# Moving part of a small projection from one norm's wait to another's, and widening a layer norm's statistic

## The reference

```python
for i in range(2):
    h += 0.5 * post1(swiglu_1(pre1(h)))           # 1024 -> 2816 -> 1024
    h += post2(mixer(pre_m(h)) @ w_o)             # three branches, one with a layer norm
    h += 0.5 * post3(swiglu_2(pre2(h)))
    gate = sigmoid(pre3(h) @ w_ple_gate)          # 1024 x 1024
    h += post4((p[i] @ w_ple_proj) * gate)        # p: the embedding, 320 x 256
y = final(h)
# the mixer's third branch: silu(layernorm(dwconv31(glu))) @ w_cf_out
```

## Time and profile before

| | |
|---|---|
| three runs, median | 1551.94 us |
| the profiled execution | 1550.16 us, its span 1548.2 us |
| TensorE matmuls | 1531.0 us busy, 99% |
| VectorE, ScalarE, GpSimd busy | 67%, 46%, 42% |
| TensorE's granted clock, mean | 0.997 |
| moved by DMA | 229.31 MB, 148 GB/s |

### The profile page before, as it was taken

One profiled execution on the slowest core, in us unless ns is written; L12 is line 12 of the kernel. 1 busy time (PEld: TensorE's weight loads), 2 busy tenths in 40 slices (PEclk: granted clock), 3 DMA queues, 4 the chain that ended last, 5 costly groups with the idle time before them and its releaser, 6 DMA issues.

```text
span 1548.2 us, 28024 instructions
## 1 busy us (share of the span) xinstructions
PE 1531.0 (99%) x10408; PEld 1521.9 (98%) x10408; DVE 1034.7 (67%) x1588; ACT 713.4 (46%) x1057; POOL 643.5 (42%) x680
## 2 busy tenths in 40 slices
PE   9999999999999999999999999999999999999997
PEld 9999999999999999999999999999999999999997
DVE  7655437999876755634885553389997866555356
ACT  6333435445456433433653333355455554334346
POOL 3755203499330655500047551035973307554001
PEclk9999999999999999999999999999999999999998
DMA  6545432444443544632334454334444335445412
GB/s 221 170 154 181 172 129 84 163 151 148 163 137 109 187 161 137 226 141 93 123 125 167 144 193 169 119 110 141 159 153 148 118 128 191 157 142 213 146 70 82
DMA packets 52921, 229.31 MB, mean 148 GB/s; under 512 B 3824, under 2 KB 3952, under 8 KB 48496
## 3 DMA queue, kind: packets, MB, share of 16 engines
q1 hardware_dynamic: 52272, 226.07, 42.6%
q10 hardware_dynamic: 576, 2.26, 0.4%
HBM read 225.27 MB, written 3.04 MB: 147 GB/s over the span
## 4 chain that ended last, share of the span: by engine, by line
PE 92%; DVE 3%; issue 2%; ACT 1%; DMA 1%; POOL 0%; SPq 0%; DVEq 0%; POOLq 0%; ACTq 0%
PE ps L449 29%; PE ps L451 29%; PE ps L450 29%; PE ps L487 1%; PE ps L491 1%; PE ps L488 1%; DVE h L1184 0%; DVE w_lo_sb L1139 0%; DVE ga L1179 0%; PE ps L553 0%; DMA raw<-in_w_f_up 0%; DMA h<-in_x 0%; DVE x_lo L1194 0%; DVE ssq L1153 0%; PE ps L562 0%
## 5 line engine op out<-in xcount | busy, mean ns | idle before, releaser
L1139 DVE TENSOR_TENSOR w_lo_sb<-raw,w_hi_sb 128x1024 fp32r<-128x1024 f32 (+1 forms) x388 | 552.4, 1424 | 229.2 <-ACT w_hi_sb L812 228.5
L449 PE MATMUL ps<-x_hi,w_hi_sb 128*128 128x320 f32 x2232 | 693.1, 311 | 1.2 <-DVE w_lo_sb L1139 1.2
L451 PE MATMUL ps<-x_hi,w_lo_sb 128*128 128x320 f32 x2232 | 689.6, 309 | 0.0
L450 PE MATMUL ps<-x_lo,w_hi_sb 128*128 128x320 f32 x2232 | 689.6, 309 | 0.0
L812 ACT ACTIVATE w_hi_sb<-raw 128x1024 fp32r<-128x1024 f32 (+1 forms) x388 | 428.9, 1110 | 558.2 <-PE ps L451 465.0
L449 PEld LDWEIGHTS ps<-x_hi,w_hi_sb 128*128 128x128 f32 x2232 | 418.9, 188 | 3.2 <-DVE w_lo_sb L1139 1.1
L450 PEld LDWEIGHTS ps<-x_lo,w_hi_sb 128*128 128x128 f32 x2232 | 419.0, 188 | 0.6
L451 PEld LDWEIGHTS ps<-x_hi,w_lo_sb 128*128 128x128 f32 x2232 | 418.9, 188 | 0.0
L450 PE MATMUL ps<-mid_lo,w_hi_sb 128*128 128x320 f32 x704 | 217.4, 309 | 0.0
L449 PE MATMUL ps<-mid_hi,w_hi_sb 128*128 128x320 f32 x704 | 217.4, 309 | 0.0
L451 PE MATMUL ps<-mid_hi,w_lo_sb 128*128 128x320 f32 x704 | 217.4, 309 | 0.0
(11 more groups left out here) (209 smaller groups left out, 1636.0 us busy)
## 6 DMA issues: line engine op xcount, KB each, us to landing
raw<-in_w_f_up SPq DMA_DIRECT2D x86, 1024.0 KB, 5.3
raw<-in_w_f_dn SPq DMA_DIRECT2D x32, 1408.0 KB, 6.0
raw<-in_w_gate SPq DMA_DIRECT2D x24, 1024.0 KB, 5.3
raw<-in_w_out SPq DMA_DIRECT2D x12, 1024.0 KB, 5.2
raw<-in_w_glu SPq DMA_DIRECT2D x8, 1024.0 KB, 5.2
raw<-in_w_short SPq DMA_DIRECT2D x8, 1024.0 KB, 5.2
raw<-in_w_wo SPq DMA_DIRECT2D x8, 1024.0 KB, 5.2
raw<-in_w_pg SPq DMA_DIRECT2D x8, 1024.0 KB, 5.3
```

The costliest lines, as they stand in the source:

```text
L449: pe.matmul(out, whi, rhs_hi, start=start, stop=False, skip_group_check=True)
L450: pe.matmul(out, whi, rhs_lo, start=False, stop=False, skip_group_check=True)
L451: return pe.matmul(out, wlo, rhs_hi, start=False, stop=stop, skip_group_check=True)
L1139: dve.tensor_tensor(w_lo_sb[:, j, 0:n], raw[:, j, 0:n], w_hi_sb[:, j, 0:n].bitcast(F32), ALU.subtract).then_inc(w_lo, 1)
```

## The change

Three parts. (1) Tiles 0 to 2 of the projection are made at post2 instead of post3. Their weights (768 of 2048 columns) have a DMA, a split and semaphores of their own: SP issues it ahead of wo's loads, into bg; ScalarE and VectorE split it in wo's first pair into y0_hi and y0_lo. Tile 0 takes the place of the three filling matmuls between post2's sums and spread, tiles 1 and 2 that of the nine behind it. VectorE copies tile 0 between its reciprocal and the wait for the spread, ScalarE tiles 1 and 2 ahead of chase. The late part has five tiles: 3 and 4 before post3's sums, 5 between sums and spread, 6 and 7 behind it; VectorE copies 3 to 5, ScalarE 6 and 7 ahead of chase. (2) The sums of pre3 move from the fourth half of pg's first pair to (0, 2) of its second pair, and its spread from (0, 1) to (0, 6). (3) Layer norm's statistic becomes wide, kept in pmf.

```diff
-        PROJ_BANKS = (4, 5, 6, 3, 2, 0, 1, 3)
+        PROJ_BANKS = (0, 1, 2, 4, 5, 6, 3, 2)
-        SPREAD = ("post1", "ln", "post2", "post3", "pre3", "post4")
-        WIDE = (None, "pre1", "pre2")
+        SPREAD = ("post1", "post2", "post3", "pre3", "post4")
+        WIDE = (None, "pre1", "ln", "pre2")
...
# SP
+                    if ph == "wo":
+
+                        sp.wait_ge(moved, v_moved(L, "out1", DT - 1))
+                        sp.dma_start(early_raw, w_proj[bass.ds(L, 1), :, 0:EARLY_W].rearrange("a p n -> (a p) n")).then_inc(early_proj_in, 16)
...
# TensorE, first_pair
-                    if ph == "pg" and k == 5:
-                        if L == LAST:
-                            turn_h(0)
-                            turn_h(1)
-                        sums(L, "pre3")
+                    if ph == "pg" and k == 5 and L == LAST:
+                        turn_h(0)
+                        turn_h(1)
...
-                pair_of_x(L, "gate2", 0, v_moved(L, "gate2", 0), {2: sums, 3: spread}, "ln")
+                pair_of_x(L, "gate2", 0, v_moved(L, "gate2", 0), {2: wide_sums}, "ln")
...
                 sums(L, "post2")
-                keep_warm(WARM_ROOT)
+                pe.wait_ge(early_proj_split, L + 1)
+                pe.wait_ge(f_out, v_f(L, 1, DT - 2))
+                project(L, 0)
                 spread(L, "post2")
-                keep_warm(WARM_X, T // 2)
+                for q in range(1, EARLY):
+                    project(L, q)
                 first_pair(L, "f2_up", v_x(L, "b2", -1), (1, L, "b2"))
+                pe.wait_ge(early_dve, L + 1)
+                pe.wait_ge(early_act, (L + 1) * (EARLY - 1))
...
                 pe.wait_ge(proj_split, L + 1)
-                for q in (0, 1):
-                    project(q)
+                for q in (EARLY, EARLY + 1):
+                    project(L, q)
                 sums(L, "post3")
-                project(2)
+                project(L, EARLY + 2)
                 spread(L, "post3")
-                for q in range(3, DT):
-                    project(q)
+                for q in range(EARLY + 3, DT):
+                    project(L, q)
...
-                pair_of_x(L, "pg", 1, ..., inside={(0, 1): spread, (2, 0): turn_rest_of_h} if L == LAST else {(0, 1): spread})
+                pair_of_x(L, "pg", 1, ..., inside={(0, 2): sums, (0, 6): spread, (2, 0): turn_rest_of_h} if L == LAST else {(0, 2): sums, (0, 6): spread})
...
# ScalarE, chase
+                if n == 1:
+                    for q in range(1, EARLY):
+                        keep_product(L, q)
                 if n == 2:
-                    keep_product(L, 3)
-                    keep_product(L, 4)
+                    for q in range(DT - PROJ_ACT, DT):
+                        keep_product(L, q)
...
-                    if n == 2 and m + 4 < DT:
-                        keep_product(L, m + 4)
...
-                        finish_root(L, "ln")
+                        wide_root(L, "ln")
...
# ScalarE, wo
+                        if (pair, j) == (0, 1):
+                            act.wait_ge(early_proj_in, L * 16 + 16)
+                            act.activation(early_hi, early_raw, ACT.Copy).then_inc(early_proj_hi, 1)
...
# VectorE, boundary
                 invert(L, post)
+                if n == 1:
+                    keep_product(L, 0)
                 if n == 2:
-                    keep_product(L, 2)
+                    keep_product(L, EARLY + 2)
...
# VectorE, layer norm
-                        invert(L, "ln")
+                        invert_all(L, "ln")
...
-                dve.wait_ge(bc_full, v_bc(L, "ln"))
+                dve.wait_ge(rinv_ready, v_stat(L, "ln"))
                 for t in range(WT):
-                    dve.tensor_tensor(cc[:, t, :], cc[:, t, :], bc, ALU.mult).then_inc(ln_step, 1)
+                    dve.tensor_tensor(cc[:, t, :], cc[:, t, :], pmf[:, :], ALU.mult).then_inc(ln_step, 1)
...
# VectorE, wo
+                        if (pair, j) == (0, 1):
+                            dve.wait_ge(early_proj_hi, L + 1)
+                            dve.tensor_tensor(early_lo, early_raw, early_hi.bitcast(F32), ALU.subtract).then_inc(early_proj_split, 1)
```

More of the change, by code:

```diff
@@ L168, in trunk @@
         FIRST_BANKS = (4, 5, 6, 3)
-        PROJ = DT * PT * P
-        proj_raw = gate[:, :, :].rearrange("p k t -> p (k t)")[:, 0:PROJ]
+        EARLY = 3
+        EARLY_W = EARLY * PT * P
+        PROJ = (DT - EARLY) * PT * P
+        early_hi = y0_hi[:, :, :].rearrange("p k t -> p (k t)")[:, 0:EARLY_W]
+        early_lo = y0_lo[:, :, :].rearrange("p k t -> p (k t)")[:, 0:EARLY_W]
+        early_raw = bg[:, :, :].rearrange("p k t -> p (k t)")[:, 0:EARLY_W]
+        proj_raw = gate[:, :, :].rearrange("p k t -> p (k t)")[:, EARLY * T:EARLY * T + PROJ]
         proj_hi = x_hi[:, :, :].rearrange("p k t -> p (k t)")[:, 0:PROJ]
         proj_lo = x_lo[:, :, :].rearrange("p k t -> p (k t)")[:, 0:PROJ]
-        PROJ_BANKS = (4, 5, 6, 3, 2, 0, 1, 3)
+        PROJ_BANKS = (0, 1, 2, 4, 5, 6, 3, 2)
         PROJ_DVE = 3
+        PROJ_ACT = DT - EARLY - PROJ_DVE
         POOLW_OUT = (ps[:, 5, 0:T], ps[:, 6, 0:T], bc, ps[:, 0, 0:T])
@@ L209, in trunk @@
         x0_hi = sem("x0_hi")
+        early_proj_in = sem("early_proj_in")
+        early_proj_hi = sem("early_proj_hi")
+        early_proj_split = sem("early_proj_split")
+        early_dve = sem("early_dve")
+        early_act = sem("early_act")
         proj_in = sem("proj_in")
@@ L301, in x_over_proj @@
         def x_over_proj(L, m):
-            return L * DT + min(DT, 2 * (((m + 1) * T - 1) // (2 * PT * P) + 1))
+            return L * DT + min(DT, EARLY + ((m + 1) * T - 1) // (PT * P) + 1)
         def v_sig(L, name, m):
@@ L578, in spread, with project @@
                 mm.then_inc(bc_full, 1)
+            def project(L, q):
+                whi, wlo, at = (early_hi, early_lo, q) if q < EARLY else (proj_hi, proj_lo, q - EARLY)
+                out = ps[:, PROJ_BANKS[q], 0:T]
+                for k in range(PT):
+                    c = (at * PT + k) * P
+                    ph, pl = p_hi[:, k * T:(k + 1) * T], p_lo[:, k * T:(k + 1) * T]
+                    pe.matmul(out, whi[:, c:c + P], ph, start=k == 0, stop=False)
+                    pe.matmul(out, whi[:, c:c + P], pl, start=False, stop=False)
+                    mm = pe.matmul(out, wlo[:, c:c + P], ph, start=False, stop=k == PT - 1)
+                mm.then_inc(proj_done, 1)
             def down(L, ph, banks_left, which, n):
@@ L766, in _ @@
                 down(L, "f2_dn", v_moved(L, "f2_up", 4 * PAIRS["f2_up"] - 3), 1, 2)
[L768 to L781, removed]
                 pe.wait_ge(proj_split, L + 1)
-                for q in (0, 1):
-                    project(q)
+                for q in (EARLY, EARLY + 1):
+                    project(L, q)
                 sums(L, "post3")
-                project(2)
+                project(L, EARLY + 2)
                 spread(L, "post3")
-                for q in range(3, DT):
-                    project(q)
+                for q in range(EARLY + 3, DT):
+                    project(L, q)
                 pe.wait_ge(proj_dve, L * PROJ_DVE + PROJ_DVE)
                 first_pair(L, "pg", v_x(L, "b3", -1), (2, L, "b3"))
-                pair_of_x(L, "pg", 1, v_moved(L, "pg", 4), stat="pre3", banks_free=True, inside={(0, 1): spread, (2, 0): turn_rest_of_h} if L == LAST else {(0, 1): spread})
+                pair_of_x(L, "pg", 1, v_moved(L, "pg", 4), stat="pre3", banks_free=True, inside={(0, 2): sums, (0, 6): spread, (2, 0): turn_rest_of_h} if L == LAST else {(0, 2): sums, (0, 6): spread})
                 if L < LAST:
@@ L828, in wide_root @@
                 act.wait_ge(stat_full, v_stat(L, name))
-                act.activation(rb[:, :], bc, ACT.Sqrt, bias=eps[:, 0:1], scale=1.0 / D).then_inc(root_ready, 1)
+                e, scale = (eps[:, 1:2], 4.0 / D) if name == "post3" else (eps[:, 0:1], 1.0 / (W if name == "ln" else D))
+                act.activation((pmf if name == "ln" else rb)[:, :], bc, ACT.Sqrt, bias=e, scale=scale).then_inc(root_ready, 1)
             def keep_rb(L, name):
@@ L1157, in invert, with invert_all @@
                 dve.reciprocal(rinv[:, :], root[:, :]).then_inc(rinv_ready, 1)
+            def invert_all(L, name):
+                dve.wait_ge(root_ready, v_stat(L, name))
+                row = (pmf if name == "ln" else rb)[:, :]
+                dve.reciprocal(row, row).then_inc(rinv_ready, 1)
             def keep_product(L, q):
                 dve.wait_ge(proj_done, L * DT + q + 1)
-                dve.tensor_copy(gate[:, q, :], ps[:, PROJ_BANKS[q], 0:T]).then_inc(proj_dve, 1)
+                dve.tensor_copy(gate[:, q, :], ps[:, PROJ_BANKS[q], 0:T]).then_inc(early_dve if q < EARLY else proj_dve, 1)
             def ple_h(i):
@@ L1198, in boundary @@
                 if n == 2:
-                    keep_product(L, 0)
-                    keep_product(L, 1)
```

(5 more changed lines are left out.)

11 lines of the change are left out of this document (5 added, 6 removed).

## The result

The kernel after takes 1554.95 us (median of 13 runs, 1553.32 to 1557.89), the kernel before 1551.18 (13 runs, 1550.37 to 1556.65). The ratio is 1.0019 with a 95% interval of 1.0011 to 1.0028: slower by 2.9 us (1.7 to 4.3). (The two medians lie 3.8 apart. The ratio is not that of the medians; it agrees with that of the means, to which one long execution of the kernel before, 1556.65, belongs.) It lies about on the 0.2% that the prediction had drawn as its bound, and certainly above nothing. The profiled execution took 1553.77, its span is 1551.7 against 1548.2, so 3.5 us have to be found in the trace.

A forecast was written before the change was run, and what follows sets the result against it. TensorE, 99% busy, was taken to bound by matmul count, except layer 0's VectorE/ScalarE chain around the embedding. Terms -0.92 + 0.72 + 1.55 + 1.15 = +2.5 us gave 1554.4, range 1550.2 to 1557.8.

The forecast's parts named there:

- Layer norm: Wide statistic replaces thin sums and spread on TensorE: 0.46 us less per layer, -0.92 for two.
- rival 4: Layer norm's whole wide reciprocal comes through and stalls out2: +1.3 us a layer, 1557.0; chance 0.04.
- Post2: At norm post2, six filling matmuls instead of three before the spread, and VectorE's copy: +0.36 us per layer, +0.72.
- Early load and split: The early tiles' weight load and its split by ScalarE and VectorE cost nothing, being taken up by waits.
- The chain to the last x_lo: VectorE's chain behind post3's step, layer 0: 10.66 us as at post2 instead of 11.08, so 0.42 earlier.
- first_pair: Behind post3, layer 0: ends at 744.22 instead of 745.96, but TensorE then waits 1.45 us for pair 1's split.
- pre3: Layer 0: sums behind the split wait come 1.65 us later, spread and first move 1.55 late, none given back: +1.55.
- rival 2: No change: the tails behind pre3 take up most of the delay, about 0, 1552 us; chance 0.14.
- Layer 1: Same delay in layer 1: spread +1.51 us, less 0.36 the last sigmoid had waited for TensorE: +1.15.
- Rival 1: TensorE sets the window's end, so first_pair's 1.74 us per layer stay gained: -3.7, 1548.2 us; chance 0.12.
- Rival 3: The clock falls in the longer wait before post4, layer 0, slowing following matmuls: 1.5 us, total +4.0, 1555.9; chance 0.25.
- The forecast's own list: Signs expected in the profile after: split waits about 1.5 and 1 us, first move 1.5 later, clock 1.00 ending layer 0.

The follow-up runs named there:

- e5: The kernel before with only layer norm's statistic made wide; 1550.38 us, ratio 0.9992.
- e2: The kernel after with VectorE's split of pg's pair 1, half 0 moved ahead of the fifth of eight additions; 1552.37 us, ratio 1.0006.
- e6: The kernel after with pre3's sums directly behind the fourth half of pg's first pair and the spread at (0, 1); 1547.88 us, ratio 0.9979.
- e4: The kernel after with 24 filling matmuls instead of six ahead of post4's sums; 1554.45 us, ratio 1.0022.
- e1: The kernel after with pre3's sums and spread back in their old places, early tiles and wide layer norm kept; 1551.17 us, ratio 1.0000.
- e7: The kernel before with only pre3's sums moved behind the fourth half of pg's first pair; 1552.01 us, ratio 1.0007.
- e3: The kernel before with only pre3's sums and spread moved to (0, 2) and (0, 6) of pg's second pair; 1555.11 us, ratio 1.0025.
- e8: The kernel after with pre3's sums behind the fourth half, spread at (0, 1), and 11 filling matmuls instead of six; 1548.19 us, ratio 0.9978.

## Why the prediction came out right, point by point

The forecast was 1554.4 with a sum of +2.5; the kernel took 1554.95, and the profiles differ by 3.5, of which 0.81 is start-up; the 2.7 left are near the sum. That the total is within 0.6 us is in part luck. The sum was put on a median of three runs, 1551.94, which is 0.8 above the median of thirteen, while the kernels' medians lie 3.8 apart and not 2.5; the two errors offset each other in part. What can be called right is the steps:

- **Layer norm, -0.46 a layer.** -0.46 and -0.43 in the lags, -0.45 in e5. out2 did not wait for y_lo, so rival 4 fell.
- **Post2, +0.36 a layer.** The first step lags 0.38 more in layer 0, and the lag grows by 0.36 up to post3's sums in layer 1. VectorE's copy at 492.42 lies between, as forecast.
- **Early load and split, nothing.** The lags between the layer norm and post2 hold nothing but the -0.46.
- **The chain to the last x_lo, 0.42 shorter.** From first step to last x_lo it is 742.61 - 731.97 = 10.64, against 11.08: 0.44.
- **first_pair, 1.74 shorter, and lost.** The end of the pair was forecast 1.74 earlier, and the wait behind it 1.45 long, to 749.2, which with the lag of 0.70 is 749.9. The wait was 1.30, to 749.90. The split came when it was forecast, and the half before it ended 0.15 later.
- **pre3, +1.65 for the sums and +1.55 for spread and first move.** Measured against the lag at the first step: 750.88 - 748.51 - 0.70 = +1.67, 753.30 - 751.04 - 0.70 = +1.56, and +1.56 for the move. The tail up to post4 gave nothing back: +1.56 there too, and rival 2 fell with it.
- **Layer 1, +1.51 for the sums, +1.15 in the end.** The wait for the split was forecast at about 1 us and was 0.84. 1519.10 - 1515.20 - 2.35 = +1.55, and +1.07.

**Rival 1** named a time that can be had, 1548.2, but by the wrong condition: that pair 1's first half were split by 747.75. e2 does that (746.17 + 1.22 = 747.39) and comes to 1552.37, for the split then stands in front of the additions, and the spread behind twelve matmuls. e6 gets 1547.88 by the place of sums and spread on TensorE. That this is near rival 1's figure is luck: it took 1.74 us off each layer, and the stretches of e6 with pre3 in them are 1.07 and 1.33 shorter than before.

**Rival 3** had a chance of 0.25 and came true in its mechanism, not in its size. The forecast's own list wanted a clock of 1.00 at the end of layer 0, and that was wrong. In the profile the fall cost 0.73 at post4, half of the 1.5 that I took, and 0.58 were given back by post1 of layer 1; e4, which keeps the clock up, is not faster by any amount that the runs can tell. The error was to price the matmuls behind the wait and not to ask whether there is slack behind them. There is: in the kernel before TensorE waits 1.10 us before 772.39 and 0.27 before 774.21 for tiles of h, and in the kernel after, at half rate, both waits are gone. All executions together, by the mean clock of each, speak for a tie between the fall and the long wait:

| kernels | wait before post4's sums, layer 0 | executions | with mean clock 0.996 or more |
|---|---|---|---|
| before | 0.58 | 61 | 27 |
| e5 | 0.59 | 11 | 5 |
| e1 | 0.58 | 11 | 4 |
| e6 | 0.82 | 11 | 7 |
| e7 | 1.05 | 11 | 3 |
| after, e2, e3 | 2.77 to 2.78 | 33 | 0 |
| e4 (after, wait filled) | none | 8 | 4 |
| e8 (e6, wait filled) | none | 11 | 8 |

With the long wait no execution kept the higher mean; with a short one about half do. So the kernel before, too, probably falls in some executions, though its one profile has no fall there; e5's profile shows it behind a wait of 0.59. The mean is a rough sign only, since it takes in the start and the end of the span too: the profile of e6, with a fall at post4, and that of e4, with none, both have 0.996. In the kernel before the two kinds take the same time (1551.17 and 1551.30, medians of 27 and 34).

What the sum did not have is the start-up: the 0.81 there. Most likely it belongs to the execution and not to the change, see below.

## What to carry to other kernels

Of the places tried here for a thin sum in the stream of a busy engine, the best was the one where its input has just become ready, behind the work that can be done while waiting for it, and ahead of the next wait for something else. With 1.3 us of wait and six matmuls before the sums, and nine matmuls more between sums and spread, -3.3 us turned into +2.9. When work is moved out of a window, look for the instruction that stands behind the next wait and move that too: here neither the tiles nor the place brought a gain alone that the times can tell. And price a clock fall by what follows it: here 0.73 us were lost, and 0.58 came back in the phase behind.

## What was not expected of the hardware

**The clock can fall behind a short wait.** In e1 it fell to half behind 1.50 us of wait before 747.71 (TensorE was busy throughout from 744 to 746, at 1.00); in the kernel after a wait of 1.30 near the same place, and in e7 one of 1.62 before 22.89, left it at 1.00. In e5 it fell behind waits of 0.59 and 0.40 with thin work between, where the same instructions in the profile of before kept 1.00. By the Trainium skill (TensorE: Matmul & The Clock Gate, "HAM oscillation — how this bites in real kernels") a wait that goes on long enough brings the half rate for the next burst; the profiles with 2.8 us (after, e2, e3) show it. But even that wait is shorter than the page's rule asks for, and e1 and e5 show the fall behind much shorter ones, so here the measurement decides. What decides between them stays open.

**Start-up differs by execution.** The first norm, pre1 in layer 0, is the same code in all these kernels, and TensorE waits before it for the first splits, fed by a DMA that is busy throughout (share 0.78 to 1.04 from 4 to 20 us in e8). In the profile of before that wait is 0.83 us. In e8's, an execution that took 1550.67 where the median of e8 is 1548.19, it is 2.25, and the clock fell behind it, as TensorE's timeline of e8 and its stretches show:

```profile
23.75 0.41 PE L466 MATMUL ps<-x_hi,w_hi_sb 128*128 128x320 f32 x1 [2.25 <-DVE w_lo_sb L1163]
```

```profile
20.00:24.00 4.00, 1.75 (x12) 1.00 0.47 194
24.00:28.00 4.00, 4.00 (x16) 0.57 0.36 93
```

All that follows stands 3 us later than in e6 (sums of post2 at 492.66 against 489.69). The sums of post1 in layer 0, up to which e1, e6 and e8 have the same code, start at 240.41, 241.35 and 244.22; in the kernel before it is 240.61, in the kernel after 241.46. So a part of the spread of one kernel's times can come from there, and two profiles should be compared from a mark behind it.

**Left open:** why e4, with the clock at 1.00, isn't faster than the kernel after (what takes its 0.4 us between post1 and post2 of layer 1 was not looked for), whether e6 would gain more with the sigmoid's table load out of the way of rb, and whether the split of e2 would pay with the sums and spread of e1. The last two were not tried.
